# Third block of a fused three-block kernel: 24 of the background gate slices placed in the scan instead of beside the decay rows and the norms

## What is computed

```python
proj = h @ w_in                       # pool_in, qkv, z, beta_raw, a_raw, gate_a, gate_b
y_a = multiscale_pool(pool_in)
q, k, v = silu(conv(qkv)); q, k = l2norm(q) * 128**-0.5, l2norm(k)       # 8 heads of 128
beta, g = sigmoid(beta_raw), -exp(a_log) * softplus(a_raw + dt_bias)     # the decay rows
# chunks of 64 tokens, 8 in all; per chunk and head:
#   a = I + strict(kb k^T * decay), attn = q k^T * decay, u, w = solve(a, ...)
# the scan over the 8 chunks:
#   v_new = u - w S;  o = qg S + attn v_new;  S = S exp(gl) + kg^T v_new
o = rms_norm(o) * o_norm_w * silu(z)            # z gate: 8 tiles of 128 features
mixed = sigmoid(gate_a) * y_a + sigmoid(gate_b) * y_b     # y_b = o; gate_b: 8 tiles
h = layer_norm(alpha * h + mixed @ w_out); then an MLP and a gated embedding
```

## Time and profile before

| | us |
|---|---|
| median of 3 runs (lowest, highest) | 3611.22 (3601.39, 3617.31) |
| the profiled execution: own time | 3615.51 |
| its span in the trace | 3613.7 |
| PE busy | 3304.1 (91%) |
| DVE busy | 1746.7 (48%) |
| ACT busy | 1216.6 (34%) |
| POOL busy | 145.5 (4%) |
| mean granted clock | 0.937 |

### The profile page before, as it was taken

One profiled execution on the slowest core, in us unless ns is written; L12 is line 12 of the kernel. 1 busy time (PEld: TensorE's weight loads), 2 busy tenths in 40 slices (PEclk: granted clock), 3 DMA queues, 4 the chain that ended last, 5 costly groups with the idle time before them and its releaser, 6 DMA issues. The chain is left out here.

```text
span 3613.7 us, 43046 instructions
## 1 busy us (share of the span) xinstructions
PE 3304.1 (91%) x17800; PEld 2606.9 (72%) x17800; DVE 1746.7 (48%) x2642; ACT 1216.6 (34%) x1751; POOL 145.5 (4%) x176
## 2 busy tenths in 40 slices
PE   8999997888699998998999999986977789999998
PEld 6888776667478886876557788865855668778885
DVE  4447536543354456767865333243643334553434
ACT  3333342222533333333443323232345222342323
POOL 0000000120000000000000000000002431000000
PEclk9999997869899999999999999998987988899999
DMA  3336321000223363322012233322220000223332
GB/s 135 97 96 216 111 79 35 2 2 8 82 71 99 117 204 128 97 79 64 1 49 86 82 95 98 99 64 64 88 88 18 19 25 20 75 82 99 94 99 94
DMA packets 76371, 285.23 MB, mean 79 GB/s; under 512 B 8464, under 2 KB 8592, under 8 KB 75152
## 3 DMA queue, kind: packets, MB, share of 16 engines
q1 hardware_dynamic: 76176, 282.47, 24.1%
HBM read 276.15 MB, written 6.29 MB: 78 GB/s over the span
## 5 line engine op out<-in xcount | busy, mean ns | idle before, releaser
L149 DVE TENSOR_TENSOR wlo<-raw,whi 128x1024 fp32r<-128x1024 f32 x450 | 552.2, 1227 | 1238.3 <-ACT whi L144 1238.0
L144 ACT ACTIVATE whi<-raw 128x1024 fp32r<-128x1024 f32 x450 | 475.9, 1058 | 1174.8 <-PE ps L173 1110.6
L171 PE MATMUL ps<-h_hi,wlo 128*128 128x512 f32 x1536 | 621.0, 404 | 51.2 <-PEq L80 21.2
L172 PE MATMUL ps<-h_lo,whi 128*128 128x512 f32 x1536 | 603.5, 393 | 0.0
L173 PE MATMUL ps<-h_hi,whi 128*128 128x512 f32 x1536 | 603.2, 393 | 0.0
L171 PEld LDWEIGHTS ps<-h_hi,wlo 128*128 128x128 f32 x1536 | 291.7, 190 | 130.6 <-issue 54.1
L172 PEld LDWEIGHTS ps<-h_lo,whi 128*128 128x128 f32 x1536 | 292.1, 190 | 62.0 <-issue 5.2
L173 PEld LDWEIGHTS ps<-h_hi,whi 128*128 128x128 f32 x1536 | 291.6, 190 | 62.0
L171 PE MATMUL ps<-mid_hi,wlo 128*128 128x512 f32 x784 | 307.4, 392 | 0.0
L173 PE MATMUL ps<-mid_hi,whi 128*128 128x512 f32 x784 | 305.0, 389 | 0.0
L172 PE MATMUL ps<-mid_lo,whi 128*128 128x512 f32 x784 | 305.0, 389 | 0.0
(11 more groups left out here) (580 smaller groups left out, 5135.9 us busy)
## 6 DMA issues: line engine op xcount, KB each, us to landing
raw<-in_wstream SPq DMA_DIRECT2D x453, 512.0 KB, 3.5
mod_ring<-in_wmod SPq DMA_DIRECT2D x48, 512.0 KB, 4.5
c_rows<-in_c_rows SPq DMA_DIRECT2D x3, 1024.0 KB, 5.6
x<-in_x_t SPq DMA_DIRECT2D x4, 512.0 KB, 7.7
x_saved<-x SPq DMA_DIRECT2D x1, 2048.0 KB, 8.9
x<-x_saved SPq DMA_DIRECT2D x1, 2048.0 KB, 9.1
mix_saved_d<-x SPq DMA_DIRECT2D x1, 2048.0 KB, 8.4
out<-x SPq DMA_DIRECT2D x8, 256.0 KB, 2.1
```

The lines of the kernel that those rows point to most:

```text
L144: act.activation(k.whi[:, n % SPLIT, :], k.raw[:, n % RAW, :], ACT.Copy).then_inc(k.hi_ready, 1)
L149: dve.tensor_tensor(k.wlo[:, n % SPLIT, :], k.raw[:, n % RAW, :], k.whi[:, n % SPLIT, :].bitcast(F32), ALU.subtract).then_inc(k.split_read ...
L171: pe.matmul(out, wlo, hi, start=first, stop=False)
L172: pe.matmul(out, whi, lo, start=False, stop=False)
```

## The change

Both the decay rows and the norms have no background slice any more, and each update of the scan has 4, 3 and 1 slices in its three gaps instead of 3, 2 and 0. The number of slices stays 128 (before 8 + 16 + 64 + 40, after 0 + 0 + 64 + 64). Chunks 0 to 7 now run beside the matrices and inversions, where chunks 3 to 10 ran, and chunks 8 to 15 in the scan, chunk j + 8 in update j, whose eighth slice is the one in gap 2.

```diff
-            gate_rows(k, ba, beta, nbeta, g, egc, ekg, egl, bg, 8)
+            gate_rows(k, ba, beta, nbeta, g, egc, ekg, egl, bg, 0)
         norm_tiles(k, [qkv[:, t, :] for t in range(16)], lambda n: (P ** -0.5 if n < 8 else 1.0), 1.0, 1e-6,
-                   bg=bg, slices=4)
+                   bg=bg, slices=0)
...
         delta_scan_and_close(k, q, key, k_tok, v_tok, xt, attn, beta, egc, egl, v, gate, h, mix_d, p_d, out, bg,
-                             (3, 2, 0))
+                             (4, 3, 1))
```

## The result

The changed kernel takes 3620.19 us (median of 20 runs, 3608.64 to 3625.34), the kernel before 3612.42 in the same comparison (20 runs, 3601.39 to 3617.31). The ratio is 1.0022 with a 95% interval of 1.0011 to 1.0032: slower by 0.2%, clear of noise but within 0.5%. The profiled execution has an own time of 3621.47 and a span of 3619.6 us, 5.9 more than before.

A forecast was written before the change was run, and what follows sets the result against it. Norms were taken as bound by ACT, the scan by PE. Terms -3.5 - 0.3 + 17.2 - 2.4 + 0.7 - 10.4 + 3.9 = +5.2 us, median 3611.2 to 3616.4; own range 3609 to 3624, 8 in 10 3604 to 3630.

The forecast's parts named there:

- Decay rows: 0: Decay rows: no change, since the slices lay in PE's wait for DVE's chain; bounds 0 and -0.3 us.
- Norms: -3.5: Norms: ACT loses 2.9 us in group 2, transposes begin 1.9 earlier, half-clock sums cost 1.3; bounds -4.8 and -3.1.
- the two gains: Norms: 2.9 us less on ACT at group 2's end, and 1.9 us from transposes beginning earlier at the stage's end.
- the loss of 1.3 for sums that begin at half clock: Norms: without slices keeping the clock up, two groups can lose 0.8 us each; 1.3 of 1.6 was taken.
- Transposes and matrices: -0.3: Matrices and inversions: three chunks become Silu, without DVE's product of 0.69 us, mostly covered by barriers; bounds -1 and 0.
- Scan without the clock: +17.2 - 2.4 + 0.7 = +15.5: Scan: added slices and gap 2's fragment cost 17.2 us, removed stalls before vn save 2.4, new waits for r0 cost 0.7.
- the sign of being wrong that I had named: Scan: a stall in front of L3222 of over 0.5 us would show the forecast wrong.
- The clock in the scan: -10.4: Scan: half-clock loss falls from 14.4 to 4 us, long stretches gone, a few short ones left; bounds -14.4 and +19.9.
- thin them to 0.6: Scan: the new slices cut the loss from short half-clock falls, 2.3 us each, to 0.6 of that.
- The rival in which the clock falls as before: Scan: small matmuls bring the clock down as often, 14.4 us of loss stay, 3626.8 us; chance 0.16.
- Tail: +3.9: From L3240's end to the merge: gate products wait for the last gate tile, 10.8 us instead of 6.85; bounds 3 and 5.
- The rival of a wait behind each table load: ACT in the scan: another wait behind each table load delays r0, 10.2 us more, 3626.6 us; chance 0.02.

The follow-up runs named there:

- the second profile: The changed kernel run once more, unedited, for another profile: 3610.76 us, with 17.0 us at half clock in the scan.
- e2: Against the changed kernel, 4, 4, 0 slices in every update of the scan instead of 4, 3, 1: 3617.85 us, ratio 1.0015 to the kernel before.
- e1: Against the changed kernel, only the last update's slices are 5, 3, 0 instead of 4, 3, 1: 3618.02 us, ratio 1.0019 to the kernel before.
- e8: Against the changed kernel: 8 slices beside the rows, 3, 3, 4 in the matrices, scan 2, 2, 0 six times and 4, 4, 0 twice: 3598.11 us, ratio 0.9952.
- e5: Against the changed kernel, 8 slices beside the decay rows again, 3, 3, 1 in every update of the scan: 3622.77 us, ratio 1.0019.

## Why the prediction was right, and where it was not

The forecast was +5.2 us and 3616.4; the measured difference of medians is +7.8, and 5.9 between the profiled executions. The sign holds in both, and so does "within 0.5%". Point by point:

- **Decay rows: 0**, right: 21.0 us in all 14 profiles, with 0 or 8 slices.
- **Norms: -3.5**, measured -5.0. The mechanism was right and the size off: the two gains came (4.8), but of the loss of 1.3 for sums that begin at half clock only 0.5 came, in group 2, and group 3 won 0.8 the same way. The clock was still up when groups 3 and 4 began, although PE had been idle for 4.80 us.
- **Transposes and matrices: -0.3**, measured -4.6. I had read that the same gaps end chunks and stopped there. The Sigmoid chunks cost more than their product on DVE: where one followed Silu chunks a table load of 1.28 us stood at the end of a round, and the round was 0.9 us longer by it. The clock was left out of this term: the matrices' half-clock time fell by 6.8 us, up to 3.4 us of time by an estimate, and the 64 transposes took 8.82 us instead of 9.68 with less of it.
- **Scan without the clock: +17.2 - 2.4 + 0.7 = +15.5**, measured +16.0, and +17.8 by the second profile. The waits: PE's idle time in the scan went from 2.4 to 1.2 us, where I had 0.7 in place of 2.4. L3222 waited 0.67 and 0.52 us at full clock where I had up to 0.4, in two updates of the first profile and in four of the second (2.4 in all): the sign of being wrong that I had named, a stall of over 0.5 us, did show.
- **The clock in the scan: -10.4**, measured -3.9 (half of 35.2 less half of 27.4), and -9.1 in the second profile. This is the step that was mis-sized: "the two long stretches to go and of the short kind to remain a few". The long ones went, and in all profiles they stand only behind waits for vn, as I had taken them. Of the short kind one came in each of updates 2 to 6, 24.0 us at half clock and 12.0 of loss where I had 4; in the second profile it was 6.8. That the new slices would thin them to 0.6 is not borne out: every fall but the start's begins between L3238 and L3214, two of them in the new slice itself, and e2, with no wait at all, has 30.6 us at half clock. The rival in which the clock falls as before was 10.4 above the forecast, and 6.5 of that came.
- **Tail: +3.9**, measured +3.65, and back at 6.84 when the last chunk ends one gap earlier (e1).

The scan's clock cost 6.5 us more than forecast and rows to matrices gave 5.8 more than forecast, so the total came out near by luck in part: two errors of opposite sign. The rule of the Trainium skill that I set beside the sum (page "TensorE: Matmul & The Clock Gate", "Part 1: The HAM clock gate": back to half speed after an idle stretch) would have made it -14.4 for the clock. The rows of e2 disagree with it: six falls after the start, and PE never idle. The rival of a wait behind each table load is out: behind the load at 2983.85 the Sigmoid begins at 2985.14, as the load ends, the product follows as counted, and the last tile was through 4.7 us after L3240 against 4.8 worked out without it. The Trainium skill, page "ScalarE: Activation LUTs", section "What ACT_TABLE_LOAD costs", would have a drain there; the trace disagrees.

## What to carry to other kernels

Ask of each gap what ends last in it: slices in a stage bound by another engine are free there, but a chunk's end (split, table load, evacuation) costs where it stands on the queue of the engine that bounds the stage, as on ACT in the norms (2.9 us in group 2 and 1.9 at the end); beside the decay rows it was free. Before moving work into a stage that is bound by TensorE, look for an intermediate one: here the matrices took 24 slices for 3.4 us, the scan for 16.0. Don't put the last unit of background work behind the last step of the main chain.

## What was not expected of the hardware

- The granted clock fell to 1.2 GHz with TensorE busy for 142.88 of 142.90 us (e2), each time in L3240 or L3214 (matmuls of 64 or 128 columns), and was back by the end of L3214 or by the matmuls of 512 columns that follow it.
- Two executions of one program had 4.4 and 21.4 us at half clock in the same scan (e8), and two of another 27.4 and 17.0 (the changed kernel). A difference of under 10 us in one stage with such matmuls can't be read from one profile.
- Taking eight slices out of such a scan won nothing clear of noise (e5, ratio 1.0019 against 1.0022): in the one profile the time that TensorE was spared came back as half-clock time.
- The stretches of 10.2 us at half clock, four in 14 profiles, all began 2.3 to 2.9 us after a wait of 0.7 to 1.5 us in front of L3229, in the short matmuls behind it.
